# Three-pass products for the second block's branch and output projections, and 128 keys for the first 128 queries

## The reference, cut to what matters

```python
h = rms_norm(x, norm_mix_g);  proj = h @ w_in                      # 1024 -> 8192
ya = moba_attention(qa, ka, va)        # 8 heads of 64; causal, since one block holds all 256 keys
xr = causal_dwconv(rx);  yb = rg_lru(xr, ...) * gelu(rgate)        # recurrent branch, 1024 wide
yc = diff_attention(qc, kc, vc)        # 4 heads, two maps each, causal, per-head norm; 512 wide
merged = g0 * (ya @ w_branch_a) + g1 * (yb @ w_branch_b) + g2 * (yc @ w_branch_c)
x = x + merged @ w_out
h = rms_norm(x, norm_ffn_g)
x = x + (gelu(u_gate) * u_val) @ ffn_down      # u = causal_dwconv(h @ ffn_up)
```

## Time and profile before

| | |
|---|---|
| median of three timed executions | 1829.77 us |
| the profiled execution's own time | 1826.0 us |
| its span, first to last instruction | 1824.2 us |
| TensorE (PE) busy | 1778.4 us, 97% |
| PE weight loads (PEld), overlapping PE | 1591.8 us, 87% |
| VectorE (DVE) busy | 1245.2 us, 68% |
| ScalarE (ACT) busy | 996.1 us, 55% |
| GpSimd (POOL) busy | 160.4 us, 9% |
| mean granted TensorE clock | 0.995 of full speed |
| HBM | 155 GB/s over the span |

### The profile page before, as it was taken

One profiled execution on the slowest core, in us unless ns is written; L12 is line 12 of the kernel. 1 busy time (PEld: TensorE's weight loads), 2 busy tenths in 40 slices (PEclk: granted clock), 3 DMA queues, 4 the chain that ended last, 5 costly groups with the idle time before them and its releaser, 6 DMA issues.

```text
span 1824.2 us, 34110 instructions
## 1 busy us (share of the span) xinstructions
PE 1778.4 (97%) x11684; PEld 1591.8 (87%) x11684; DVE 1245.2 (68%) x2493; ACT 996.1 (55%) x2008; POOL 160.4 (9%) x136
## 2 busy tenths in 40 slices
PE   7999999999999999999999999999899999999998
PEld 1878789998899987888899999999799899899997
DVE  3786466663489979766766666666776666248887
ACT  2545543341166689766655555555567657036666
POOL 0000014310284420000000000000000000010000
PEclk9999999999999999999999999999999999999999
DMA  8523223234455421355555555555364533455553
GB/s 294 185 99 105 85 89 105 86 122 134 144 186 177 170 90 43 117 191 192 195 187 188 189 184 184 187 188 189 117 218 144 169 121 124 150 179 186 188 185 127
DMA packets 77269, 283.30 MB, mean 155 GB/s; under 512 B 8576, under 2 KB 8576, under 8 KB 76928
## 3 DMA queue, kind: packets, MB, share of 16 engines
q1 hardware_dynamic: 77184, 282.16, 45.9%
HBM read 281.08 MB, written 1.05 MB: 155 GB/s over the span
## 4 chain that ended last, share of the span: by engine, by line
PE 84%; DVE 10%; ACT 3%; issue 1%; DMA 1%; POOL 1%; PEld 0%; PEldq 0%; POOLq 0%; SPq 0%; DVEq 0%; ACTq 0%
PE banks L853 19%; PE banks L841 16%; PE banks L436 7%; PE banks L1070 7%; PE banks L932 7%; PE banks L777 5%; PE banks L1094 3%; PE banks L627 2%; PE banks L608 2%; DVE split L2186 2%; PE banks L1044 2%; PE banks L805 2%; DVE arena L2182 1%; PE banks L404 1%; PE banks L616 1%
## 5 line engine op out<-in xcount | busy, mean ns | idle before, releaser
L1382 ACT ACTIVATE split<-arena 128x512 fp32r<-128x512 f32 x492 | 309.0, 629 | 135.0 <-PE banks L841 76.9
L841 PEld LDWEIGHTS banks<-split 128*128 128x128 f32 x2880 | 355.4, 192 | 10.5 <-DVE split L2114 3.1
L853 PE MATMUL banks<-split 128*128 128x512 f32 x1536 | 361.9, 390 | 1.0 <-issue 1.0
L841 PE MATMUL banks<-split 128*128 128x256 f32 x2880 | 358.8, 283 | 3.1 <-DVE split L2114 2.3
L2204 DVE TENSOR_TENSOR split<-arena,split 128x512 fp32r<-128x512 f32 x396 | 270.5, 690 | 105.4 <-ACT split L1382 99.6
L853 PEld LDWEIGHTS banks<-split 128*128 128x128 f32 x1536 | 283.8, 188 | 57.2 <-issue 1.4
L1363 ACT ACTIVATE split<-arena 128x512 fp32r<-128x512 f32 x264 | 164.5, 627 | 104.1 <-PE banks L1070 52.3
L932 PE MATMUL banks<-split 128*128 128x256 f32 x1344 | 169.9, 287 | 3.9 <-DVE split L2283 3.9
L932 PEld LDWEIGHTS banks<-split 128*128 128x128 f32 x1344 | 165.4, 194 | 7.0 <-issue 6.6
L436 PEld LDWEIGHTS banks<-split 128*128 128x128 f32 (+1 forms) x936 | 131.9, 191 | 28.9 <-issue 13.9
L436 PE MATMUL banks<-split 128*128 128x256 f32 (+2 forms) x936 | 150.8, 319 | 5.1 <-DVE split L1755 3.4
(11 more groups left out here) (396 smaller groups left out, 2465.2 us busy)
## 6 DMA issues: line engine op xcount, KB each, us to landing
arena<-wstream SPq DMA_DIRECT2D x525, 512.0 KB, 3.3
arena<-x_t SPq DMA_DIRECT2D x1, 2048.0 KB, 12.8
arena<-matsa SPq DMA_DIRECT2D x1, 1234.0 KB, 6.5
out_t<-arena SPq DMA_DIRECT2D x4, 256.0 KB, 2.0
arena<-mats SPq DMA_DIRECT2D x1, 576.0 KB, 8.2
arena<-crow SPq DMA_DIRECT2D x1, 512.0 KB, 7.3
arena<-rows SPq DMA_DIRECT2D x1, 512.0 KB, 4.9
arena<-mats SPq DMA_DIRECT2D x1, 449.0 KB, 3.8
```

The lines of the kernel that those rows point to most:

```text
L841: mm = pe.matmul(ps[:, 4 + b, 0:S], w_parts[:, c, (2 * m + half) % 4, P * k:P * k + P], h_parts[:, e, 4 * half + k, :], start=(half == 0 a ...
L853: mm = pe.matmul(ps[:, 2 * tt + half, :], g_parts[:, e, j % 2, P * tt:P * tt + P], w_parts[:, c, (2 * m + half) % 4, :], start=(first and ...
L1382: act.activation(w_parts[:, 0, (2 * m + half) % 4, :], ring[:, peer_slot(m), 512 * half:512 * half + 512], ACT.Copy).then_inc(sem["w_hi"], 1)
```

## The change

It does three things.

1. Groups 0, 1, 4 and 5 of the attentions use 128 keys (`keys_of`): scores, bias, maximum, exponentials, scaling, transposes and value products alike. The four score products are issued in the order 0, 1, 2, 3.
2. The 16 branch tiles and eight output tiles become three-pass tiles 320 to 343 of the same split chain, whose order is now: recurrent 0 and 1, attention 0 to 7, recurrent 2 to 7, output 0 to 7. The activations are split too: the recurrent output in rounds 4 to 7 (`recurrent_lo`), both attention outputs around the phase's end (`heads_hi`, `heads_lo`, 128x1024 each), the merged branches piece by piece (`merged_hi`, `merged_lo`). Their parts lie where `hp`, `h_parts` and `g_parts` lay; the feed-forward part uses `ff_parts` and `ffg_parts`. Merges are divided in `recurrent_merge` and `attention_merge`. The recurrent tile 0 runs between input tile 63 and the turning of the last heads. The four sigmoids stand between the splits.
3. Loads of these tiles wait for splits, not for matmuls; semaphores `hp_hi`, `hp_lo` are counted in `h_hi`, `h_lo` (`H_AT` gives the offsets); the tiles' order in memory is changed.

```diff
+keys_of = lambda g: P * (g // 2 % 2 + 1)
+REC_BANKS = (0, 1, 4, 5)
 # SyncE
-            load_freed_by_parts(N_IN2 + RING, N_BR2 + RING, M_IN2)
-            load_freed_by_matmuls(N_BR2 + RING, N_FFN + RING)
+            load_freed_by_parts(N_IN2 + RING, N_FFN + RING, M_IN2)
 # TensorE
+            def recurrent_branch(d):
+                if d < 4:
+                    pe.wait_ge(sem["o_moved"], 3 + d)
+                else:
+                    pe.wait_ge(sem["rec_used"], d - 3)
+                full_parts(M_BR2 + (d if d < 2 else 8 + d), rg_parts, ps[:, REC_BANKS[d % 4], 0:S])
+            def attention_branches(d):
+                ...   # for each half: waits for w_lo and h_lo of its heads, 4 k x 3 passes into its half of a bank
             in2_tile(63)
+            pe.wait_ge(sem["h_lo"], H_AT["rec"] + 4)
+            recurrent_branch(0)
             for qt in range(2):
                 pe.wait_ge(sem["o2_ready"], qt + 1)
                 turn_heads(1, qt, 4 + qt)
             phase_end(pe, 4)
+            recurrent_branch(1)
             for d in range(KT):
+                attention_branches(d)
+            for d in range(2, KT):
+                recurrent_branch(d)
             for d in range(KT):
-                full(N_OUT2 + d, y2T, 4 + d % 4, ...)
+                full_parts(M_OUT2 + d, y2_parts, ps[:, (2, 3, 6, 7)[d % 4], 0:S], ...)
 # ScalarE, round g >= 4, ahead of the next exponentials
+                    act.activation(rg_parts[:, 0, 2 * c:2 * c + 2, :], rgl[:, 2 * c:2 * c + 2, :], ACT.Copy).then_inc(sem["h_hi"], 1)
 # ScalarE, behind the eight rounds (tiles 64 and 65 are split by in2_out(62), in2_out(63))
+            act.wait_ge(sem["o_moved"], 4)
+            heads_hi(0)
             ...   # moves the last heads
+            act.wait_ge(sem["o_moved"], 6)
+            heads_hi(1)
             phase_end(act, 4)
+            for x in range(16):
+                if x in (0, 2, 4, 6):
+                    act.activation(branch_gates[:, :, x:x + 2, :], branch_gates[:, :, x:x + 2, :], ACT.Sigmoid)...
+                tile_used(M_BR2 + x, 0)      # waits until TensorE is done with the half, then part_hi(m + 2, half)
+                tile_used(M_BR2 + x, 1)
+                if x == 7:
+                    act.activation(small[:, 84:85], eps, ACT.Sqrt)
+                if x == 9:
+                    for d in range(2):
+                        merged_hi(d)
+                if x > 9:
+                    merged_hi(x - 8)
 # VectorE, end of round g
-                for half in range(2):
-                    in2_lo(a + 4, half)
+                if g < 7:
+                    for half in range(2):
+                        in2_lo(a + 4, half)
                 ...   # moves the outputs of group g
                 if g < 4:
                     rg_merge(g)
+                else:
+                    recurrent_lo(g - 4)
 # VectorE, behind the scaling of the last heads
+            heads_lo(0)
+            for half in range(2):
+                in2_lo(65, half)
+            heads_lo(1)
             phase_end(dve, 4)
+            def recurrent_merge(d):
+                ...   # d < 2: y = bank * gate; else t = bank * gate, y = y + t
+            def attention_merge(d):
+                ...   # two products with the gates and one sum; for d < 2 two sums
+            for x in range(16):
+                in2_lo(64 + x + 2, 0)
+                ...   # recurrent_merge(x), attention_merge(x - 2) or recurrent_merge(x - 8)
+                in2_lo(64 + x + 2, 1)
+                ...   # merged_lo: pieces 0 and 1 at x == 9, x - 8 after it
             for d in range(KT):
                 dve.wait_ge(sem["tiles_done"], N_OUT2 + d + 1)
                 ...   # residual
+                in2_lo(80 + d + 2, 0)
                 if d:
                     weighted_lo(d - 1)
+                in2_lo(80 + d + 2, 1)
             weighted_lo(KT - 1)
```

More of the change, by code:

```diff
@@ L59 @@
 MATA_AT = dict(zip(MATSA, np.cumsum([0] + list(MATSA.values())).tolist()))
+PARTS_OF = dict(proj=2 * KT, expert=4, in2=KT, rec=4, heads=2, merged2=KT, ff=KT)
+H_AT = dict(zip(PARTS_OF, np.cumsum([0] + list(PARTS_OF.values())).tolist()))
 SEMS = """params_in x_in late_in out_written tiles_done phase
-silu_c mod_bank_free mod_cols squares square_sums sums roots normed v_turned scaled hp_hi hp_lo in_hi in_lo in_used
+silu_c mod_bank_free mod_cols squares square_sums sums roots normed v_turned scaled in_hi in_lo in_used
 proj_free conv_done conv_used ab_moved ab_ready ab_exp decay_in decay_sums decay_ready decay_made
@@ L988, in turn2 @@
                 for n, t in enumerate(ts):
-                    for c in range(2):
+                    for c in range(keys_of(g) // P):
                         mm = pe.transpose(ps[:, 4 + q % 2, S * n + P * c:S * n + P * c + P], lg[:, g % 2, t, P * c:P * c + P], ident)
@@ L1000, in weigh2 @@
                     o = 64 * t if g < 4 else P * (t // 2)
-                    for c in range(2):
+                    last = keys_of(g) // P - 1
+                    for c in range(last + 1):
                         mm = pe.matmul(ps[:, 6 + g % 2, o:o + m], tn2[:, q % 2, n, c, :], v2[g // 4][:, c, at0:at0 + m],
-                                       start=(c == 0), stop=(c == 1))
+                                       start=(c == 0), stop=(c == last))
                 mm.then_inc(sem["weighted"], 1)
@@ L1033, in _ @@
             phase_end(pe, 4)
+            recurrent_branch(1)
             for d in range(KT):
[L1037 to L1047, removed]
+                attention_branches(d)
+            for d in range(2, KT):
+                recurrent_branch(d)
             for d in range(KT):
-                full(N_OUT2 + d, y2T, 4 + d % 4, (sem["resid"], 2 * KT + d - 3) if d >= 4 else None, KT if d == 0 else None)
+                full_parts(M_OUT2 + d, y2_parts, ps[:, (2, 3, 6, 7)[d % 4], 0:S], (sem["resid"], 2 * KT + d - 3) if d >= 4 else None,
+                           H_AT["merged2"] if d == 0 else None)
             def turn_residual(tt):
@@ L1093, in ffn_down @@
                         for c, e in PASSES:
[L1094 removed]
+                            mm = pe.matmul(ps[:, 2 * tt + half, :], ffg_parts[:, e, f % 2, P * tt:P * tt + P],
                                            w_parts[:, c, (2 * (M_FFN + x) + half) % 4, :], start=False, stop=False,
```

195 lines of the change are left out of this document (124 added, 71 removed).

## The result

The changed kernel takes 1815.82 us, the median of four executions (1813.05 to 1816.85). The kernel before takes 1829.25 beside it (1825.90 to 1831.47). The ratio is 0.993 with a 95% interval of 0.9918 to 0.9942, so 10.6 to 15.0 us are gone. The prediction was 1815.7.

What follows compares the result with a forecast made beforehand. The prediction took PE, busy 97% of the span, as the bound. Its terms, -14.15+2.6+1.3+0.3-2.6-0.35-1.0-0.2, summed to -14.1 us, taking the median from 1829.77 to 1815.7 us, range 1810.5 to 1821.5.

Steps and rivals of the forecast that it cites:

- Three passes: Branch and output projections: 24 tiles go from 3.465 to 2.875 us each, -14.15 us.
- Rival (e): Three-pass instructions start 109.2 ns apart, the skill page's pace, not 119.6; 1809.6 us, chance 0.02.
- The splits keep up: Run of projection tiles: VectorE needs 2.55 to 2.65 of 2.87 us a tile, so no stall inside the run.
- Rival (a): VectorE becomes the bound at 3.3 us a tile in the sixteen branch tiles; 1822.7 us, chance 0.13.
- Rival (b): Merge and split stand in series with PE, 4.12 us a branch tile; 1835.7 us, chance 0.06.
- The loop: Attention loop: 128 keys give -2.6, -0.35 and -1.0 us, and rounds 4 to 6 -0.2.
- Rounds 0 and 1 and the start: Attention loop: fewer transposes and value products in groups 0 and 1, -2.6 us; shorter wait for group 0's logits, -1.0.
- The halved scores of groups 4 and 5: Attention scores: eight instructions go from 1.07 us to 0.87 or 0.54, counted once on the path, -0.35 us.
- rounds 4 to 6: Attention loop: VectorE's chain loses 2.3 us and gains 2.1 in three recurrent remainders, -0.2 us.
- The phase's end: Between input and branch projections: splitting the attention heads ahead of it leaves PE idle 3.8 us, +2.6 us.
- The start of the branches: Behind the phase's end: sigmoid table, sigmoid and third tile's first split take 4.15 us against 2.87 of cover, +1.3.
- The join: Last output tile to feed-forward part: VectorE's last remainder is ready at T+2.9, due at T+2.5, +0.3 us.

Runs made afterwards that it cites:

- e6: The changed kernel with one extra 128x256 VectorE product, result unused, in each of the last 14 branch tiles; 1811.34 us, a single execution.
- e9: The same kernel as e6, timed over four executions; 1814.39 us, ratio 0.9924 to the kernel before.
- e7: The changed kernel with two extra 128x256 VectorE products, results unused, in each of 14 branch tiles; 1819.52 us, a single execution.
- e1: The kernel before with only the 128 keys for groups 0, 1, 4 and 5; 1822.20 us, ratio 0.9969.
- e2: The changed kernel with 256 keys in all groups, so projections and splits alone; 1819.86 us, ratio 0.9962.
- e3: The changed kernel with 27 unused dummy products on PE ahead of the barrier at the phase's end; 1811.36 us, ratio 0.9905.
- e4: The changed kernel with PE not waiting at the phase's end, tiles 65 and 66 split earlier and each sigmoid behind a split; 1812.65 us, ratio 0.9913.
- e5: The changed kernel with the recurrent remainders of rounds 4 to 7 on GpSimd instead of VectorE; 1813.50 us, ratio 0.9917.
- e10: The changed kernel as it is, timed and profiled again; 1816.14 us, ratio 0.9937 to the kernel before.

## Why the prediction was right

- **Three passes, -14.15.** Right, 2.885 us a tile, by a pace read off the same instruction form elsewhere in the trace. Rival (e), 109.2 ns an instruction, would have given 2.62 us a tile; no run of tiles here has it.
- **The splits keep up.** Right, and with less margin used than thought. Rival (a) took VectorE at 3.3 us a tile; it is 16.86 x 2.885/19.00 = 2.56 us a tile, the 2.55 to 2.65 of the working. That 92% is no bound is shown by e6 and e9, at 98%; that the bound exists, by e7. Rival (b), merge and split in series with PE, is out by the same runs: 0.42 us in that series would have cost 5.9.
- **The loop.** Rounds 0 and 1 and the start as worked out. The halved scores of groups 4 and 5 both stand on the path, at the seams of rounds 2 and 3 and of rounds 3 and 4, where I counted one; at 0.65 us for eight they lie between my two ends (0.87, 0.54), below the 0.72 I took. For rounds 4 to 6 the sum held and its parts did not: I had 2.3 gained against 2.1 paid. e1 shows 1.06 gained; the changed kernel stands at +0.12, so 1.18 was paid. In e2, where nothing was spared, the same remainders cost 1.79 (40.56 in place of 38.77). So 1.06 of the 2.3 that VectorE is spared reach the path, and 1.2 to 1.8 of the 2.1 that it is given. That PE's own work is close behind would explain it; no run here takes PE's work away. GpSimd can take the remainders for about 0.7 us.
- **The phase's end, +2.6.** Right at +2.27: 3.32 us idle where 3.8 was worked out. One reading under it was off: tile 63's row ends at 1541.60 (1538.49 + 3.11), so before the phase ended 1.94 us behind it, not 2.15, and the working should have given +2.8.
- **The start of the branches, +1.3: the step that failed.** Its size was off by a factor of two, and its mechanism was not the one named. I had the sigmoid's table load, the sigmoid, and then the third tile's first split in series behind the barrier. The table load runs ahead of the barrier, and no more than 0.23 us of stall is left (e3). In the kernel before, ScalarE itself came to the barrier last (1543.54), so its table load at 1543.56 looked as if it had waited for the barrier. What cost the time instead was the granted clock, which fell to 0.50 behind the idle time that the step before had put there: +2.6. The prediction had read the clock as 1.00 in its windows and put its fall at nothing, though it forecast a new idle time of 3.8 us in the paragraph before. e3 shows the cause: the barrier where it was, PE busy, and the cost gone. With the stall at 0.23 and no fall of the clock the sum would have been -15.2, further off: the 1.3 us for a stall that did not come stood in, by luck, for half of a cost that was not foreseen; with both the term is 2.6 in place of 1.3 (the 5.49 holds the stall), and the sum is -12.8.
- **The join, +0.3.** Right at +0.43, PE idle 0.5 us for the last remainder.

So the total is right within 1.1 us: one term was too cheap by 1.3, the others' misses were at most 0.5 and partly cancelled. That the medians agree within 0.1 us (1815.82 and 1815.7) is luck as well, since the four executions lie 3.8 us apart. What stays open: how often the timed executions of the change see the fall behind the barrier, since their mean clock mixes it with the others.

## What to carry to other kernels

Where an exact split frees the bound engine, price the helpers by whether each result is there before its turn, not by their busy share: here VectorE went to 98% without cost and to a loss one operation later. A barrier put behind a new chain costs its idle time and can cost as much again by the clock (2.6 us behind 3.3 here); ask of each new idle time on TensorE what runs behind it, and move independent work in, or even useless products. For a new path ahead of a barrier, check which of the instructions behind it (a table load) can run before it opens.

## What the runs showed of the hardware

- The granted clock fell to 0.50 behind 3.3 us of idle time in six of seven traces, and stayed there for up to 5.5 us of the work behind it. It fell once behind 2.01 us (e7), and twice, in e4 and e5, behind only 1.18 and 0.92 us with eight small products between, and did not in seven other traces with those idle times (after, e1, e3, e6, e7, e9, e10). A fall cost 1.6 to 2.6 us. One and the same idle time gave 5.49, 4.45 and 3.14 us for one tile. By the Trainium skill, "TensorE: Matmul & The Clock Gate", section "Part 1: The HAM clock gate (the "warmup" mystery)", how many matmuls run at the lower clock differs from run to run of one kernel; the page says it of a kernel's start. e9 and e6, one kernel with 4.45 and 3.14, agree with it in the middle of one.
- A table load ran ahead of the barrier that its activation waited for: 1545.76 against 1547.03. In e4 it started at 1550.62, as soon as the copy ahead of the sigmoid was done. Whether the engine or the compiled order puts it there is not shown.
- Eight score products with 128 keys (64x128) take 0.65 us in the rounds, 81 ns each; sixteen products with values take 1.73, 108 ns each.
